# Stick-breaking attention: masks added by TensorE, logs summed as two float32r parts by single products

## The chip, the cores and the metric

The kernel runs on one core of a Trainium2 chip. The metric is the device time of one execution in microseconds (us). Three executions of the kernel before took 1486.97, 1491.43 and 1493.3 us; the median is 1491.43 us. The row tables and the trace come from one more execution under the profiler: 1495.53 us, of which the instructions span 1494.1 us, so 1.4 us lie around the span.

## The reference, cut to what matters

Two transformer blocks on 256 tokens of width 1024 are computed. The change touches one part of the first block, the stick-breaking attention of 16 heads of dimension 64. Its core is

```python
z = einsum('bhtd,bhsd->bhts', q * 64 ** -0.5, k)
causal = s < t                                  # strict
log_1mb = where(causal, log_sigmoid(-z), 0.0)
tail = cumsum(log_1mb, axis=s, reverse=True)
w = where(causal, exp(z + tail), 0.0)
out = einsum('bhts,bhsd->bhtd', w, v)
```

For each query t and key s the weight is exp of the score plus the sum of the logs of all keys from s to t. The work around it that matters here: the projections q, k, v before it, a gate projection `ga` of the same input that shares TensorE with the attention, and the projection `att` of the attention's output after it.

## The kernel before, in words

**Weights.** All weight matrices come in pieces of 128 x 2048 numbers. SyncE loads a piece into `raw` (4 slots); ScalarE rounds it to float32r (`w_hi`, `act_split`, L433); VectorE forms the rest, raw minus w_hi (`w_lo`, `dve_split`, L443); TensorE multiplies with three float32r products per tile (`three`, L453 to L455). Which engine splits which piece at which place is written out by hand in the program of each engine. Each engine runs its program in order, and semaphores (`wait_ge`, `then_inc`) are the only coupling.

**The attention stage** (`pe_stick`, `act_stick`, `dve_stick`) handles the 16 heads as 8 pairs j = 0 to 7, keys on the partitions, queries along the free axis. A pair's scores are 2 heads x 384 columns (key block 0 with 256 queries, key block 1 with the last 128), in PSUM, double buffered by `stick_z` (psum_a for even j, psum_c for odd j). For pair j:

1. TensorE, `pe_stick_scores`: four plain float32 products (L729, L730), once `stick_wt(j-2)` says that the PSUM buffer has been read out.
2. VectorE, L787: L = min(z, 30). ScalarE, L765 and L767: L = ln(1 + exp(L)). VectorE, L789: L = max(z, L). VectorE, L791: L times the strict mask on the two diagonal blocks.
3. TensorE, `pe_stick_weights`: six plain float32 products (L739 to L741) add to z the sums of L, with `neg_from` (lower triangle of -1) and `neg_ones` as weights of the products.
4. ScalarE, L773: `stick_w` = exp of PSUM. VectorE, L800, twice: min with 3e38 and strict mask on the diagonal blocks.
5. TensorE, `pe_stick_output`, L757: the product with v. ScalarE L779 and VectorE L806: the output in two float32r parts `y_hi` and `y_lo`.

The three programs interleave the pairs. In round j (1 to 6) TensorE does: one gate tile (12 products of `ga`), scores of pair j+1, one gate tile, weights of pair j, output of pair j-1. ScalarE does: exp and ln of pair j+1, in rounds 1, 2, 5 and 6 the split of one weight piece, the weights' exp of pair j, `y_hi` of pair j-1. VectorE does: min, max and mask of pair j+1, in the same rounds its half of the split, the weights' mask of pair j, `y_lo` of pair j-1. Ahead of round 4 ScalarE copies out the first half of the gate (`act_gate_out`, L911 and L912), for which TensorE waits before the first gate tile of that round.

**After the rounds** TensorE does weights(7), output(6), then the first half of `att0`, output(7), the rest of `att0` and then `att1`, which waits for splits that ScalarE starts after `y_hi(7)`, the second gate copy and the gate's sigmoid (L920).

**Before the stage** TensorE waits for the small column constants (`cols`, L705). VectorE then scales a few gain columns (L2951, L2957) and enters `dve_stick`. `memory_kv` is first written much later, by `kv2`.

Of the kernel before, what the change touches and what calls it, by code (L numbers as in the profile page):

```python
# [99 lines left out]
class Kernel:  # L100
# [9 lines left out]
    def memory(self):  # L110
# [28 lines left out]

        self.stage = self.put("stage", [P, 5, P], y_hi_at)  # L140
        half = 4 * KD * SEQ
        self.stick_l = self.put("stick_l", [P, 2, 2, 384], y_hi_at + half)
        self.stick_w = self.put("stick_w", [P, 2, 2, 384], y_lo_at + half)
        self.rows = self.put("rows", [P, 2, 4, 4, P], y_lo_at)
        self.xc = self.put("xc", [P, 2, MT, GH, SSM_HD], y_hi_at)
        self.xd = self.put("xd", [P, 2, GH, SSM_HD], y_hi_at + 8192)
# [180 lines left out]
    def semaphores(self, known):  # L327
        def new(name, unit=1):
            s = Signal(self.nc, self.ctx, name, known, unit)
            self.signals.append(s)  # L330
            return s
# [15 lines left out]
        self.res_added, self.post_sq_act, self.post_gain_dve, self.post_sums, self.post_mean, self.post_root = (  # L347
            new(n) for n in ("res_added", "post_sq_act", "post_gain_dve", "post_sums", "post_mean", "post_root"))

        (self.stick_z, self.stick_min, self.stick_exp, self.stick_ln, self.stick_max, self.stick_logs, self.stick_s, self.stick_wt,  # L350
         self.stick_wm, self.stick_o, self.stick_hi, self.stick_lo) = (new("stick_" + n) for n in (
             "z", "min", "exp", "ln", "max", "logs", "s", "wt", "wm", "o", "hi", "lo"))

        self.dt_act, self.dt_dve, self.conv_act, self.conv_dve, self.conv_silu, self.xs_turned, self.xs_act, self.xs_dve = (
            new(n) for n in ("dt_act", "dt_dve", "conv_act", "conv_dve", "conv_silu", "xs_turned", "xs_act", "xs_dve"))
# [358 lines left out]
def stick_z(k, j):  # L714

    return (k.psum_a, k.psum_c)[j % 2][:, 0:1024].rearrange("p (b w) -> p b w", b=2)[:, :, 0:384]


def stick_diagonal(x):
    return x.rearrange("p b (k t) -> p b k t", t=P)[:, :, 0:3:2, :]  # L720


def pe_stick_scores(k, j):
    pe, z = k.nc.tensor, stick_z(k, j)
    if j >= 2:
        pe.wait_ge(*k.stick_wt.by(j - 2))
    for b in range(2):
        r = slice(64 * b, 64 * b + 64)
        pe.matmul(z[:, b, 0:SEQ], k.k_t[r, j, 0:P], k.q_t[r, j, :], start=True, stop=False, skip_group_check=True)  # L729
        mm = pe.matmul(z[:, b, SEQ:384], k.k_t[r, j, P:SEQ], k.q_t[r, j, P:SEQ], start=False, stop=False, skip_group_check=True)  # L730
    mm.then_inc(*k.stick_z.at(j))


def pe_stick_weights(k, j):
    pe, z, u = k.nc.tensor, stick_z(k, j), j % 2
    pe.wait_ge(*k.stick_logs.by(j))
    for b in range(2):
        L = k.stick_l[:, u, b, :]
        pe.matmul(z[:, b, 0:SEQ], k.neg_from[:], L[:, 0:SEQ], start=False, stop=False, skip_group_check=True)  # L739
        pe.matmul(z[:, b, P:SEQ], k.neg_ones[:], L[:, SEQ:384], start=False, stop=False, skip_group_check=True)  # L740
        mm = pe.matmul(z[:, b, SEQ:384], k.neg_from[:], L[:, SEQ:384], start=False, stop=True, skip_group_check=True)  # L741
    mm.then_inc(*k.stick_s.at(j))


def stick_o(k, j):

    return k.psum_b[:, 512 * (j % 2):512 * (j % 2) + SEQ]


def pe_stick_output(k, j):  # L750
    pe, u, o = k.nc.tensor, j % 2, stick_o(k, j)
    pe.wait_ge(*k.stick_wm.by(j, 1))
    if j >= 2:
        pe.wait_ge(*k.stick_lo.by(j - 2))
    for m in range(MT):
        for b in range(2):
            mm = pe.matmul(o[64 * b:64 * b + 64, P * m:SEQ], k.v_n[:, m, j * P + 64 * b:j * P + 64 * b + 64],  # L757
                           k.stick_w[:, u, b, SEQ * m:SEQ * m + SEQ - P * m], start=m == 0, stop=m == 1, skip_group_check=True)
    mm.then_inc(*k.stick_o.at(j))


def act_stick_softplus(k, j):
    act, L = k.nc.scalar, k.stick_l[:, j % 2, :, :]
    act.wait_ge(*k.stick_min.by(j))
    act.activation(L, L, ACT.Exp).then_inc(*k.stick_exp.at(j))  # L765
    act.wait_ge(*k.stick_exp.by(j))
    act.activation(L, L, ACT.Ln, bias=1.0).then_inc(*k.stick_ln.at(j))  # L767


def act_stick_weights(k, j):  # L770
    act = k.nc.scalar
    act.wait_ge(*k.stick_s.by(j))
    act.activation(k.stick_w[:, j % 2, :, :], stick_z(k, j), ACT.Exp).then_inc(*k.stick_wt.at(j))  # L773


def act_stick_output(k, j):
    act = k.nc.scalar
    act.wait_ge(*k.stick_o.by(j))
    act.activation(k.Y[0][:, j, :], stick_o(k, j), ACT.Copy).then_inc(*k.stick_hi.at(j))  # L779


def dve_stick_softplus(k, j):

    dve, z, L = k.nc.vector, stick_z(k, j), k.stick_l[:, j % 2, :, :]
    strict = k.strict[:].unsqueeze(1).unsqueeze(1).to_broadcast([P, 2, 2, P])
    dve.wait_ge(*k.stick_z.by(j))
    dve.tensor_scalar(L, z, 30.0, None, ALU.min).then_inc(*k.stick_min.at(j))  # L787
    dve.wait_ge(*k.stick_ln.by(j))
    dve.tensor_tensor(L, z, L, ALU.max).then_inc(*k.stick_max.at(j))  # L789
    dve.wait_ge(*k.stick_max.by(j))  # L790
    dve.tensor_tensor(stick_diagonal(L), stick_diagonal(L), strict, ALU.mult).then_inc(*k.stick_logs.at(j))  # L791


def dve_stick_weights(k, j):
    dve = k.nc.vector
    strict = k.strict[:].unsqueeze(1).to_broadcast([P, 2, P])
    dve.wait_ge(*k.stick_wt.by(j))
    for b in range(2):
        d = stick_diagonal(k.stick_w[:, j % 2, b:b + 1, :])[:, 0, :, :]
        dve.scalar_tensor_tensor(out=d, in0=d, scalar=3.0e38, in1=strict, op0=ALU.min, op1=ALU.mult).then_inc(*k.stick_wm.at(j, b))  # L800
# [52 lines left out]
def act_stick(k):  # L853
    k.nc.scalar.preload_act_table_set("natural_log_exp_and_others")
    act_stick_softplus(k, 0)
    act_stick_softplus(k, 1)
    act_stick_weights(k, 0)
    for j in range(1, STICK - 1):
        if j == 4:
            act_gate_out(k, 0)  # L860
        act_stick_softplus(k, j + 1)
        if j in (1, 2, 5, 6):
            act_split(k, 1)
        act_stick_weights(k, j)
        act_stick_output(k, j - 1)
    act_stick_weights(k, STICK - 1)
    act_stick_output(k, STICK - 2)
    act_stick_output(k, STICK - 1)
    act_gate_out(k, 1)


def dve_stick(k):
    dve_stick_softplus(k, 0)
    dve_stick_softplus(k, 1)
    dve_stick_weights(k, 0)
    for j in range(1, STICK - 1):
# [2050 lines left out]
def vector_program(k):  # L2927
    dve, col = k.nc.vector, k.col_of
# [19 lines left out]
    for name, l, dim in (("fox_q_gain_2", 1, HD), ("mla_q_gain_2", 1, QK), ("mem_q_gain_2", 2, HD)):  # L2948
        c = HEAD_GAINS[name]
# [173 lines left out]
```

## Time and profile before

| what | value |
|---|---|
| three executions, median | 1491.43 us |
| profiled execution | 1495.53 us |
| its span | 1494.1 us |
| TensorE busy | 1358.6 us (91%) |
| VectorE busy | 907.2 us (61%) |
| ScalarE busy | 691.4 us (46%) |
| mean granted TensorE clock | 0.948 |

Busy time is summed per engine, and the engines run beside each other. PE is TensorE, PEld its weight loads, DVE is VectorE, ACT is ScalarE, POOL is GpSimd, SP is SyncE. In a row such as `L787 TENSOR_SCALAR stick_l<-psum_a 128x768`, the line of the kernel comes first, then the operation, what it writes and reads, and its size. A bracket `[1.88 <-PE psum_c L730]` at the end says how long the engine had been idle and what released it. A plain float32 product is recorded as two matmuls, so "x4" for L729 is two products.

### The profile page before, as it was taken

The page shows a single profiled execution, that of the slowest core. Times are in us where ns is not written, and L with a number is a line of the kernel's source. Part 1 is how long each engine was busy: PE and PEld are TensorE (multiplying, and loading weights), DVE is VectorE, ACT ScalarE, POOL GpSimd, SP SyncE. Part 2 cuts the span into 40 slices and gives each one's busy share as a digit, 9 for nine tenths or more (in the row PEclk, how much of TensorE's full clock was granted, in tenths as well). Part 3 has the DMA queues.
Part 4 walks back from the last instruction along what each step waited for, and adds up shares of the span by engine and source line. Part 5 has one row for each costly group of instructions (what it writes and reads, how often), then busy time and mean ns, then how long its engine had stood idle before and what let it go on. Part 6 is the DMA issues. An engine that isn't in the chain of part 4 may idle for free.

```text
span 1494.1 us, 21370 instructions
## 1 busy us (share of the span) xinstructions
PE 1358.6 (91%) x8820; PEld 1211.9 (81%) x8820; DVE 907.2 (61%) x1295; ACT 691.4 (46%) x974; POOL 156.1 (10%) x262
## 2 busy tenths in 40 slices
PE   5999998779998988899998899799997858899998
PEld 5988998448997987799997677699996746799997
DVE  4456478655646644654545666677766478576765
ACT  4345556225625444544333554545454456445442
POOL 6000020110000000020000131000000172000000
PEclk9999999779999999899999899899998869999999
DMA  7531444103653543356565433265663320266561
GB/s 263 177 131 35 169 170 170 57 0 113 231 206 114 188 151 99 113 176 198 177 186 182 141 113 85 71 200 181 182 192 127 134 57 15 85 182 198 171 191 63
DMA packets 206400, 212.68 MB, mean 142 GB/s; under 512 B 7009, under 2 KB 151859, under 8 KB 206304
## 3 DMA queue, kind: packets, MB, share of 16 engines
q1 hardware_dynamic: 203840, 206.25, 43.2%
q0 software_dynamic: 2160, 4.02, 0.8%
q8 instruction: 70, 1.15, 0.3%
q10 hardware_dynamic: 304, 1.05, 0.2%
q14 instruction: 26, 0.21, 0.0%
HBM read 210.24 MB, written 1.05 MB: 141 GB/s over the span
## 4 chain that ended last, share of the span: by engine, by line
PE 81%; DVE 10%; ACT 5%; issue 2%; POOL 1%; DMA 0%; DVEq 0%; ACTq 0%; POOLq 0%
PE psum_a L453 10%; PE psum_b L453 10%; PE psum_a L454 10%; PE psum_a L455 10%; PE psum_b L455 10%; PE psum_b L454 10%; PE psum_c L453 5%; PE psum_c L454 4%; PE psum_c L455 4%; DVE w_lo L443 3%; PE psum_c L571 2%; ACT w_hi L433 1%; PE psum_c L1139 1%; PE psum_c L1166 1%; ACT normed_rows L554 1%
## 5 line engine op out<-in xcount | busy, mean ns | idle before, releaser
L443 DVE TENSOR_TENSOR w_lo<-raw,w_hi 128x2048 fp32r<-128x2048 f32 (+3 forms) x235 | 447.8, 1942 | 94.7 <-ACT w_hi L433 93.9
L433 ACT ACTIVATE w_hi<-raw 128x2048 fp32r<-128x2048 f32 (+3 forms) x235 | 371.8, 1620 | 32.7 <-PE psum_b L455 18.0
L453 PE MATMUL psum_a<-x_hi,w_hi 128*128 128x256 f32 x752 | 215.9, 287 | 4.8 <-DVE w_lo L443 4.8
L454 PE MATMUL psum_a<-x_lo,w_hi 128*128 128x256 f32 x752 | 214.8, 286 | 0.0
L455 PE MATMUL psum_a<-x_hi,w_lo 128*128 128x256 f32 x752 | 214.7, 285 | 0.0
L453 PE MATMUL psum_b<-x_hi,w_hi 128*128 128x256 f32 x752 | 214.2, 285 | 0.0
L455 PE MATMUL psum_b<-x_hi,w_lo 128*128 128x256 f32 x752 | 213.6, 284 | 0.0
L454 PE MATMUL psum_b<-x_lo,w_hi 128*128 128x256 f32 x752 | 213.5, 284 | 0.0
L453 PEld LDWEIGHTS psum_a<-x_hi,w_hi 128*128 128x128 f32 x752 | 146.7, 195 | 6.3 <-DVE w_lo L443 5.1
L454 PEld LDWEIGHTS psum_a<-x_lo,w_hi 128*128 128x128 f32 x752 | 146.6, 195 | 1.4
L454 PEld LDWEIGHTS psum_b<-x_lo,w_hi 128*128 128x128 f32 x752 | 145.2, 193 | 1.6
L455 PEld LDWEIGHTS psum_a<-x_hi,w_lo 128*128 128x128 f32 x752 | 146.4, 195 | 0.0
L453 PEld LDWEIGHTS psum_b<-x_hi,w_hi 128*128 128x128 f32 x752 | 145.3, 193 | 1.4
L455 PEld LDWEIGHTS psum_b<-x_hi,w_lo 128*128 128x128 f32 x752 | 145.1, 193 | 0.0
L453 PE MATMUL psum_c<-w_hi,ffn_hidden_hi 128*128 128x512 f32 x264 | 106.2, 402 | 4.1 <-DVE ffn_hidden_lo L1582 4.1
L454 PE MATMUL psum_c<-w_lo,ffn_hidden_hi 128*128 128x512 f32 x264 | 105.6, 400 | 0.0
L455 PE MATMUL psum_c<-w_hi,ffn_hidden_lo 128*128 128x512 f32 x264 | 105.6, 400 | 0.0
L1590 POOL CAST ffn_hidden_hi<-ffn_h 128x256 fp32r<-128x256 f32 x66 | 26.5, 402 | 543.2 <-DVE ffn_h L1579 369.1
L571 PE MATMUL psum_c<-ident,normed_rows 128*128 128x128 f32 x144 | 32.2, 410 | 49.1 <-ACT normed_rows L554 45.2
L571 PEld LDWEIGHTS psum_c<-ident,normed_rows 128*128 128x128 f32 x144 | 23.7, 206 | 58.0 <-DVE normed_rows L548 29.2
L453 PEld LDWEIGHTS psum_c<-w_hi,ffn_hidden_hi 128*128 128x128 f32 x264 | 50.6, 192 | 14.3 <-issue 4.9
L455 PEld LDWEIGHTS psum_c<-w_hi,ffn_hidden_lo 128*128 128x128 f32 x264 | 50.4, 191 | 12.5
(495 smaller groups left out, 2594.8 us busy)
## 6 DMA issues: line engine op xcount, KB each, us to landing
raw<-in_ffn_w_up_dram SPq DMA_DIRECT2D x88, 512.0 KB, 5.1
raw<-in_w_in_dram SPq DMA_DIRECT2D x40, 1024.0 KB, 5.9
raw<-in_w_gu_dram SPq DMA_DIRECT2D x44, 512.0 KB, 5.1
raw<-in_ffn_w_down_dram SPq DMA_DIRECT2D x44, 512.0 KB, 5.9
raw<-in_w_down_dram SPq DMA_DIRECT2D x22, 512.0 KB, 5.9
raw<-in_w_br_ssm_dram SPq DMA_DIRECT2D x8, 1024.0 KB, 5.6
raw<-in_w_xkv_dram SPq DMA_DIRECT2D x8, 1024.0 KB, 5.7
raw<-in_w_out_dram SPq DMA_DIRECT2D x8, 1024.0 KB, 5.1
```

The source lines that it names most:

```text
L433: act.activation(k.w_hi[:, s, 0:size], k.raw[:, s, 0:size], ACT.Copy).then_inc(*k.rounded.at(*key))
L443: dve.tensor_tensor(k.w_lo[:, s, 0:size], k.raw[:, s, 0:size], k.w_hi[:, s, 0:size].bitcast(F32), ALU.subtract).then_inc(*k.split.at(*key))
L453: pe.matmul(out_ap, l[0], r[0], start=start, stop=False, skip_group_check=True)
L454: pe.matmul(out_ap, l[0], r[1], start=False, stop=False, skip_group_check=True)
L455: return pe.matmul(out_ap, l[1], r[0], start=False, stop=stop, skip_group_check=True)
L554: act.activation(k.normed_rows[:, 0, :], src[:, 0, :], ACT.Copy, scale=k.squares[:, at + 2:at + 3]).then_inc(*k.scaled_act.at(tag))
L571: mm = pe.transpose(ps[:, m * P:(m + 1) * P], k.normed_rows[:, m, j * P:(j + 1) * P], k.ident[:])
L1139: pe.matmul(ssd_seg(k, q), k.beyond[:], k.rows[:, g % 2, 2 * c + q, :, :].rearrange("p h t -> p (h t)"), start=True, stop=True).then_inc(* ...
L1166: mm = pe.matmul(k.psum_c[:, at:at + SSM_HD], k.rows[:, g % 2, 2 * c + q, h, :], k.xc[:, g % 2, c, 4 * q + h, :], start=q == 0 and h == 0, ...
L1590: pool.tensor_copy(k.hid[0][:, u, :], k.h32[:, u, :]).then_inc(*k.ffn_hi.at(tag, h))
```

## The change

It changes how pairs are masked and how the logs are summed.

- **Constants.** Four 128 x 128 float32r tiles `stick_consts` (copies of `neg_from`, `neg_ones`, `ident`, and a tile of 0 and -1e30 made from `strict`) are written by VectorE ahead of `dve_stick`. TensorE waits for them ahead of its stage.
- **Scores.** Four float32r products of 128 columns, identity times mask tile, are added to the scores of each pair, and `stick_z` is signalled behind them. The maskings L791 and L800 are gone.
- **Logs.** After max, ScalarE copies L (128 x 768) to a float32r tile `stick_l_hi` (`act_stick_logs`), then VectorE writes `stick_l_lo` = L - `stick_l_hi` (128 x 768). The copy stands in ScalarE's program right behind the pair's ln, ahead of the round's split and of the weights' exp.
- **Sums.** Six plain float32 products per pair become eight float32r ones: 4 of 384 columns and 4 of 128.
- **Buffers.** `stick_l` has one buffer in place of two (in the place of `memory_kv`), so min(j) waits for the logs of j-1. `stick_w` moves, and its exp waits for output(j-2).

```diff
 def pe_stick_scores(k, j):
...
-        mm = pe.matmul(z[:, b, SEQ:384], k.k_t[r, j, P:SEQ], k.q_t[r, j, P:SEQ], start=False, stop=False, skip_group_check=True)
+        pe.matmul(z[:, b, SEQ:384], k.k_t[r, j, P:SEQ], k.q_t[r, j, P:SEQ], start=False, stop=False, skip_group_check=True)
+    for b in range(2):
+        for at in (0, SEQ):
+            mm = pe.matmul(z[:, b, at:at + P], k.stick_consts[:, 2, :], k.stick_consts[:, 3, :], start=False, stop=False,
+                           skip_group_check=True)
     mm.then_inc(*k.stick_z.at(j))
...
-        L = k.stick_l[:, u, b, :]
-        pe.matmul(z[:, b, 0:SEQ], k.neg_from[:], L[:, 0:SEQ], start=False, stop=False, skip_group_check=True)
-        pe.matmul(z[:, b, P:SEQ], k.neg_ones[:], L[:, SEQ:384], start=False, stop=False, skip_group_check=True)
-        mm = pe.matmul(z[:, b, SEQ:384], k.neg_from[:], L[:, SEQ:384], start=False, stop=True, skip_group_check=True)
+        for part in k.stick_parts:
+            pe.matmul(z[:, b, 0:384], k.stick_consts[:, 0, :], part[:, u, b, :], start=False, stop=False, skip_group_check=True)
+        for part in k.stick_parts:
+            mm = pe.matmul(z[:, b, P:SEQ], k.stick_consts[:, 1, :], part[:, u, b, SEQ:384], start=False, stop=True,
+                           skip_group_check=True)
...
-    pe.wait_ge(*k.stick_wm.by(j, 1))
+    pe.wait_ge(*k.stick_wt.by(j))
...
+def act_stick_logs(k, j):
+    act, u = k.nc.scalar, j % 2
+    act.wait_ge(*k.stick_max.by(j))
+    if j >= 2:
+        act.wait_ge(*k.stick_s.by(j - 2))
+    act.activation(k.stick_parts[0][:, u, :, :], k.stick_l[:, :, :], ACT.Copy).then_inc(*k.stick_logs_hi.at(j))
...
 def dve_stick_softplus(k, j):
...
+    if j:
+        dve.wait_ge(*k.stick_logs.by(j - 1))
     dve.tensor_scalar(L, z, 30.0, None, ALU.min).then_inc(*k.stick_min.at(j))
     dve.wait_ge(*k.stick_ln.by(j))
     dve.tensor_tensor(L, z, L, ALU.max).then_inc(*k.stick_max.at(j))
-    dve.wait_ge(*k.stick_max.by(j))
-    dve.tensor_tensor(stick_diagonal(L), stick_diagonal(L), strict, ALU.mult).then_inc(*k.stick_logs.at(j))
+    dve.wait_ge(*k.stick_logs_hi.by(j))
+    dve.tensor_tensor(k.stick_parts[1][:, u, :, :], L, k.stick_parts[0][:, u, :, :].bitcast(F32), ALU.subtract).then_inc(*k.stick_logs.at(j))
...
 def act_stick(k):
     k.nc.scalar.preload_act_table_set("natural_log_exp_and_others")
     act_stick_softplus(k, 0)
+    act_stick_logs(k, 0)
     act_stick_softplus(k, 1)
+    act_stick_logs(k, 1)
     act_stick_weights(k, 0)
     for j in range(1, STICK - 1):
         if j == 4:
             act_gate_out(k, 0)
         act_stick_softplus(k, j + 1)
+        act_stick_logs(k, j + 1)
         if j in (1, 2, 5, 6):
             act_split(k, 1)
         act_stick_weights(k, j)
```

`dve_stick` loses its calls of `dve_stick_weights` and is otherwise as before.

## Rows read from the trace of the kernel before

**Rows 1.** Page, the chain that ended last, its shares by engine.

```profile
PE 81%; DVE 10%; ACT 5%; issue 2%; POOL 1%; DMA 0%; DVEq 0%; ACTq 0%; POOLq 0%
```

**Rows 2.** Chain in time order, attention stage: start, duration (us), work.

```profile
103.67 1.91 ACT w_hi L433
105.60 2.29 DVE w_lo L443
107.89 0.67 DVE stick_w L800 x2
```

**Rows 3.** Timeline of DVE: start, duration (us), instruction, idle before and releaser.

```profile
90.99 0.23 DVE L2957 TENSOR_TENSOR head_cols<-head_cols 128x1 f32<-128x1 f32 x2
91.70 0.96 DVE L787 TENSOR_SCALAR stick_l<-psum_a 128x768 f32<-128x768 f32 x1 [0.49 <-PE psum_a L730]
96.05 0.95 DVE L787 TENSOR_SCALAR stick_l<-psum_c 128x768 f32<-128x768 f32 x1
98.79 0.96 DVE L789 TENSOR_TENSOR stick_l<-psum_c,stick_l 128x768 f32<-128x768 f32 x1 [1.79 <-ACT stick_l L767]
99.78 0.69 DVE L791 TENSOR_TENSOR stick_l<-stick_l,strict 128x512 f32<-128x512 f32 x1
101.06 0.95 DVE L787 TENSOR_SCALAR stick_l<-psum_a 128x768 f32<-128x768 f32 x1
108.48 0.41 DVE L806 TENSOR_TENSOR y_lo<-psum_b,y_hi 128x256 fp32r<-128x256 f32 x1
108.81 0.95 DVE L787 TENSOR_SCALAR stick_l<-psum_c 128x768 f32<-128x768 f32 x1
116.56 0.95 DVE L787 TENSOR_SCALAR stick_l<-psum_a 128x768 f32<-128x768 f32 x1
123.86 0.96 DVE L787 TENSOR_SCALAR stick_l<-psum_c 128x768 f32<-128x768 f32 x1 [1.88 <-PE psum_c L730]
130.51 0.96 DVE L787 TENSOR_SCALAR stick_l<-psum_a 128x768 f32<-128x768 f32 x1 [1.23 <-PE psum_a L730]
138.28 0.95 DVE L787 TENSOR_SCALAR stick_l<-psum_c 128x768 f32<-128x768 f32 x1
```

**Rows 4.** Timeline of ACT in the same stage.

```profile
97.03 0.84 ACT L765 ACTIVATE stick_l<-stick_l 128x768 f32<-128x768 f32 x1 [2.62 <-DVE stick_l L787]
97.91 0.84 ACT L767 ACTIVATE stick_l<-stick_l 128x768 f32<-128x768 f32 x1
98.66 0.79 ACT L773 ACTIVATE stick_w<-psum_a 128x768 f32<-128x768 f32 x1
105.47 0.79 ACT L773 ACTIVATE stick_w<-psum_c 128x768 f32<-128x768 f32 x1
119.17 0.79 ACT L773 ACTIVATE stick_w<-psum_c 128x768 f32<-128x768 f32 x1
```

**Rows 5.** Timeline of PE: the stage, then the first att1 product and a later mask product.

```profile
121.26 0.39 PE L453 MATMUL psum_c<-x_hi,w_hi 128*128 128x256 f32 x1 [2.10 <-ACT merged L912]
122.87 0.71 PE L729 MATMUL psum_c<-q_t,k_t 64*128 64x256 f32 x4
144.19 0.60 PE L739 MATMUL psum_c<-stick_l,neg_from 128*128 128x256 f32 x2
146.03 0.87 PE L757 MATMUL psum_b<-stick_w,v_n 128*64 128x256 f32 x8
146.84 0.39 PE L453 MATMUL psum_a<-y_hi,w_hi 128*128 128x256 f32 x1
162.54 0.39 PE L453 MATMUL psum_b<-y_hi,w_hi 128*128 128x256 f32 x1 [2.97 <-DVE w_lo L443]
879.56 0.67 PE L2168 MATMUL psum_c<-causal_r,ident_r 128*128 128x128 f32 x4
```

**Rows 6.** Windows: length; busy us of PE, PEld, DVE, ACT, POOL; granted clock; DMA.

```profile
160.00:162.00 2.00, 0.00 (x0) 0.00 (x0) 1.80 (x1) 2.00 (x3) 0.00 (x0) 1.00 0.00 0
164.00:166.00 2.00, 2.00 (x12) 2.00 (x11) 2.00 (x4) 0.00 (x0) 0.00 (x0) 0.50 0.88 319
```

More of the change, by code:

```diff
@@ L134, in memory @@
         self.rotary = self.sb("rotary", [P, 2, MT, 16])
+        self.memory_kv_at = self.top
         self.memory_kv = self.sb("memory_kv", [P, MT, 2 * MEM_W])
@@ L141, in memory @@
         half = 4 * KD * SEQ
-        self.stick_l = self.put("stick_l", [P, 2, 2, 384], y_hi_at + half)
-        self.stick_w = self.put("stick_w", [P, 2, 2, 384], y_lo_at + half)
         self.rows = self.put("rows", [P, 2, 4, 4, P], y_lo_at)
@@ L156, in memory @@
         self.v_n = self.put("v_n", [P, MT, D], at + 24576)
+        self.stick_parts = [self.put(n, [P, 2, 2, 384], o, F32R)
+                            for n, o in (("stick_l_hi", at + 32768), ("stick_l_lo", y_lo_at + half))]
+        self.stick_w = self.put("stick_w", [P, 2, 2, 384], y_hi_at + half)
+        self.stick_l = self.put("stick_l", [P, 2, 384], self.memory_kv_at)
+        self.stick_consts = self.put("stick_consts", [P, 4, P], at + 38912, F32R)
         self.gate_s = self.put("gate_s", [P, KD, SEQ], at + 8192)
@@ L348, in semaphores @@
             new(n) for n in ("res_added", "post_sq_act", "post_gain_dve", "post_sums", "post_mean", "post_root"))
-        (self.stick_z, self.stick_min, self.stick_exp, self.stick_ln, self.stick_max, self.stick_logs, self.stick_s, self.stick_wt,
-         self.stick_wm, self.stick_o, self.stick_hi, self.stick_lo) = (new("stick_" + n) for n in (
-             "z", "min", "exp", "ln", "max", "logs", "s", "wt", "wm", "o", "hi", "lo"))
+        (self.stick_z, self.stick_min, self.stick_exp, self.stick_ln, self.stick_max, self.stick_logs_hi, self.stick_logs, self.stick_s,
+         self.stick_wt, self.stick_o, self.stick_hi, self.stick_lo, self.stick_made) = (new("stick_" + n) for n in (
+             "z", "min", "exp", "ln", "max", "logs_hi", "logs", "s", "wt", "o", "hi", "lo", "made"))
         self.dt_act, self.dt_dve, self.conv_act, self.conv_dve, self.conv_silu, self.xs_turned, self.xs_act, self.xs_dve = (
@@ L716, in stick_z, with dve_stick_consts @@
     return (k.psum_a, k.psum_c)[j % 2][:, 0:1024].rearrange("p (b w) -> p b w", b=2)[:, :, 0:384]
-def stick_diagonal(x):
-    return x.rearrange("p b (k t) -> p b k t", t=P)[:, :, 0:3:2, :]
+def dve_stick_consts(k):
+    dve, c = k.nc.vector, k.stick_consts
+    for j, x in enumerate((k.neg_from, k.neg_ones, k.ident)):
+        dve.tensor_copy(c[:, j, :], x[:])
+    dve.tensor_scalar(c[:, 3, :], k.strict[:], 1.0, -NEG, ALU.subtract, ALU.mult).then_inc(*k.stick_made.at())
 def pe_stick_scores(k, j):
@@ L762, in act_stick_softplus @@
 def act_stick_softplus(k, j):
-    act, L = k.nc.scalar, k.stick_l[:, j % 2, :, :]
+    act, L = k.nc.scalar, k.stick_l[:, :, :]
     act.wait_ge(*k.stick_min.by(j))
@@ L772, in act_stick_weights @@
     act.wait_ge(*k.stick_s.by(j))
+    if j >= 2:
+        act.wait_ge(*k.stick_o.by(j - 2))
     act.activation(k.stick_w[:, j % 2, :, :], stick_z(k, j), ACT.Exp).then_inc(*k.stick_wt.at(j))
@@ L782, in dve_stick_softplus @@
 def dve_stick_softplus(k, j):
-    dve, z, L = k.nc.vector, stick_z(k, j), k.stick_l[:, j % 2, :, :]
-    strict = k.strict[:].unsqueeze(1).unsqueeze(1).to_broadcast([P, 2, 2, P])
+    dve, z, u = k.nc.vector, stick_z(k, j), j % 2
+    L = k.stick_l[:, :, :]
     dve.wait_ge(*k.stick_z.by(j))
+    if j:
+        dve.wait_ge(*k.stick_logs.by(j - 1))
     dve.tensor_scalar(L, z, 30.0, None, ALU.min).then_inc(*k.stick_min.at(j))
@@ L789, in dve_stick_softplus @@
     dve.tensor_tensor(L, z, L, ALU.max).then_inc(*k.stick_max.at(j))
-    dve.wait_ge(*k.stick_max.by(j))
-    dve.tensor_tensor(stick_diagonal(L), stick_diagonal(L), strict, ALU.mult).then_inc(*k.stick_logs.at(j))
[L794 to L800, printed above, removed]
+    dve.wait_ge(*k.stick_logs_hi.by(j))
+    dve.tensor_tensor(k.stick_parts[1][:, u, :, :], L, k.stick_parts[0][:, u, :, :].bitcast(F32), ALU.subtract).then_inc(*k.stick_logs.at(j))
 def dve_stick_output(k, j):
@@ L813, in pe_stick @@
         k.nc.tensor.wait_ge(*k.out_dve.by(unit))
+    k.nc.tensor.wait_ge(*k.stick_made.by())
     gates = pe_gate_tiles(k)
@@ L874, in dve_stick @@
     dve_stick_softplus(k, 1)
-    dve_stick_weights(k, 0)
     for j in range(1, STICK - 1):
@@ L879, in dve_stick @@
             dve_split(k, 1)
-        dve_stick_weights(k, j)
         dve_stick_output(k, j - 1)
-    dve_stick_weights(k, STICK - 1)
     dve_stick_output(k, STICK - 2)
@@ L2957, in vector_program @@
         dve.tensor_tensor(k.head_cols[:, c:c + 1], k.head_cols[:, a:a + 1], k.head_cols[:, b:b + 1], ALU.mult).then_inc(*k.scaled_gains.at(c))
+    dve_stick_consts(k)
     dve_stick(k)
```

## The prediction

> **What bounds the kernel now.** I read the chain that ended last first: TensorE has 81% of it, VectorE 10%, ScalarE 5%, DMA 0% [rows 1]. Nothing waits for data from memory, so what a stage loses on its own chain reaches the end. Then I read the chain in order of time inside the stage that the diff touches (about 91 to 147 us). There it isn't TensorE throughout: in a round with a weight split it goes through ScalarE's split, VectorE's split and VectorE's masking of the weights [rows 2]. The timeline of VectorE shows the beat of the stage. I call m(j) the start of min(j), L787. It stands at 91.70, 96.05, 101.06, 108.81, 116.56, 123.86, 130.51 and 138.28 us for j = 0 to 7 [rows 3]. Steps between them: 4.35, 5.01, 7.75, 7.75, 7.30, 6.65, 7.77. The split rounds (7.75) are VectorE's: its instructions follow each other without an idle bracket. The steps 7.30 and 6.65 end in a wait for the scores, so TensorE sets them, the first of the two through its wait of 2.10 us for the gate's copy [rows 3, 5]. From m(7) to the first `att0` product it is 146.84 - 138.28 = 8.56 us [rows 3, 5].
>
> **Prices of what moves.**
> *Scores.* From the first score product to min it is 123.86 - 122.87 = 0.99 us [rows 3, 5]. Four float32r mask products come in between. The same product stands in the fox stage: four take 0.67 us from the first start to the last end, which is 0.17 each if nothing overlaps, and (0.67 - 0.39) / 3 = 0.09 for each further one if a single one lasts 0.39 like the L453 row [rows 5]. I take 0.13, the middle: four are 0.5 us (bounds 0.37 and 0.67), and scores to min becomes 1.49.
> The Trainium skill, "TensorE: Matmul & The Clock Gate", section "Back-to-back issue gap", gives about 81 ns for each 128-column product with its weight load. By it the four would be 0.32 us, an estimate; the trace's four float32r products are slower than that, and the measured row is used.
> *Sums.* The six float32 products take 146.03 - 144.19 = 1.84 us [rows 5]. The gate tile, twelve float32r products of 256 columns, takes 122.87 - 121.26 = 1.61, so 0.13 each, as for 128 columns; 384 columns lie between 0.13 and 0.20 (half as much again), and I take 0.17. Four of each kind: 4 x 0.17 + 4 x 0.13 = 1.2, with the tail 1.3 us. TensorE saves 0.54 a pair here and pays 0.5 for the masks: its own work stays the same.
> *VectorE.* Gone per pair: mask of L, at most 0.69 us, and mask of the weights, 0.67 [rows 2, 3]. New: the subtraction of 128 x 768, at 0.96 like L789 of the same size, 0.87 until the next can start. In sum 0.4 less.
> *ScalarE.* New: a copy of 128 x 768, 0.84 like L765, 0.75 until the next starts (98.66 - 97.91) [rows 4].
>
> **Where they lie.** The copy needs max(j), and in ScalarE's program the split and the weights' exp stand behind it. From m: exp at +0.98, ln at +1.86, max at +2.74, the dependent instruction at +3.73 (99.78 - 98.79 = 0.99 later) [rows 3, 4]. Before, ScalarE was free for the split at m+2.61. Now the copy runs at +3.73 and ScalarE is free at +4.48: the split and the exp are 1.87 us later, behind a wait for VectorE's max. The subtraction starts at +4.6, and the logs are there at +5.6.
> - *Split round.* ScalarE's split starts at +4.48 and takes 1.91; VectorE's split starts at +6.4 and holds VectorE 2.2 (105.60 to 107.8) [rows 2]; y_lo takes 0.33 more (108.48 to 108.81) [rows 3]. Next min at +8.94, not 7.75: +1.19 for each of four (m2 to m3, m3 to m4, m6 to m7; the fourth split falls behind m7). VectorE's saved masks are hidden, because it now idles for ScalarE's half. Scores would be there at +4.48 + 1.80 + 0.79 + 0.05 + 1.49 = 8.6, just inside.
> - *Round without split.* Exp of the weights at +4.48, done at +5.27, scores at +5.31, next min at +6.80. For m5 to m6 that is +0.15 over 6.65. For m1 to m2 the same loop, 6.80 for 5.01: +1.79.
> - *m0 to m1.* Min(1) waits for the subtraction of pair 0: +5.6 for 4.35: +1.24.
> - *m4 to m5.* Exp of the weights at +4.48; in the trace it was at +2.61 (119.17 - 116.56), and the gate tile, the scores and min hung on it through y_hi and the gate copy. Everything shifts by 1.87, with the masks' 0.5: +2.36.
> - *Entry.* The constants are four VectorE instructions of 128 x 128 behind L2957, which ends at 91.22. Each costs between the 0.1 of a tiny one (0.23 for two) and 0.69 for 128 x 512 [rows 3]; I take 0.22, so TensorE starts at about 92.1 in place of 90.74 (0.96 ahead of 91.70, as above): +1.35. With the masks m0 is 1.85 later. Bounds 0.9 to 3.2.
> - *Exit.* From m7: scores(7) had started 1.82 before m7 (at m6 + 7.12), then TensorE needs scores 1.4, gate 1.45, sums 1.3, output 0.81, two gate tiles 2.95, sums(7) 1.3 and output(6) 0.81, in sum 10.0, so `att0` starts at m7+8.2 in place of 8.56: -0.36.
>
> Sum: 1.85 + 1.24 + 1.79 + 3 x 1.19 + 2.36 + 0.15 - 0.36 = 10.6 us later at `att0`. Behind it, the chain y_hi(7), gate copy, sigmoid, split of `att1` hangs on output(7), which moves with `att0`, so all 10.6 pass on; the single L buffer and the waits for output(j-2) and s(j-2) are met long before and cost nothing.
>
> **The clock.** TensorE's work per round is about 6.6 us, so in the longer rounds it idles 2.3 to 3.1 us at a stretch. In the trace an idle stretch of 2.97 us ahead of 162.54 was followed by a granted clock of 0.50 at 164 to 166 us, the level of 1.2 GHz, with 12 products in 2 us where 0.13 us each gives 15 [rows 5, 6]. Idle 2.10 us ahead of 121.26 did no harm that I see. If a fall lands on the gate tile and scores of m4 to m5, or on scores(2), it is on the chain; in the split rounds 0.3 us of slack covers part. I put 1.2 us on it, bounds 0 and 8. Forecast: 10.6 + 1.2 = +11.8 us. Against the profiled execution that is 1495.53 + 11.8 = 1507.3; the profiled execution lies 4.1 above the median of the three, so the time is 1491.4 + 11.8 = 1503.2 us.
>
> **Rivals.**
> A. *VectorE's load decides, not the order on ScalarE*, the case on the other side. If the copy slipped in beside other work (ScalarE is idle 2.6 us ahead of L765 [rows 4]), the split rounds would fall by the 0.4 that VectorE saves, and the stage would change by 1.85 - 3 x 0.4 = +0.6, less if the entry is hidden: 1492, within 0.5%. Against it: that idle time lies before min, and the copy needs max. It decides from the point at which ScalarE's copy ends before its split could start anyway, and the code's order excludes that. Chance 0.13.
> B. *Faster*: float32r takes the sums off TensorE as if TensorE were the bound of every round. Eight pairs times 0.54 give -4.3 if the masks hide under them; masks and entry take back 5.9. Only with nearly free masks and constants does it give 1488. 1483 would need more than the whole of the sums' 1.84 us a pair to come free. Chance 0.05, and I count 0.03 of it beyond 0.5%, for what I may have overlooked.
> C. *The clock falls in each long gap.* Five gaps (before scores(2), (3), (4), the gate tile, scores(7)), each losing up to half of 3 us = 1.5 us on the chain, 7.5 in all: 10.6 + 7.5 = +18, 1509.5 us. For it: the row of the fall; against: slack in the split rounds, and the price is full only when the fall starts with the scores. The Trainium skill, "TensorE: Matmul & The Clock Gate", section "HAM oscillation — how this bites in real kernels", tells of a loop whose every burst restarts cold because a wait precedes it; by that rule C would be the case, and the one fall behind 162.54 agrees with it. Chance 0.17.
> The forecast has 0.65.
>
> **How the numbers follow.** The forecast's own spread is about 3 us each way: entry bounds, mask price, and executions of before that differ by 6 us. The range for 8 in 10 is 1496.5 to 1511. It leaves out most of A and B and the upper edge of C. About 0.5%, 7.5 us, is what a measurement can tell from no change, so the border to slower is 1498.9. Of the forecast's 0.65 some 0.07 fall short of it, C's 0.17 lie above: slower 0.75. A's 0.13, 0.02 of B and that 0.07: same 0.22. Faster 0.03.
>
> **What would show it.** In the timeline of the changed kernel: ScalarE's Copy of stick_l_hi starting 3.7 us behind min and released by max; the w_hi split behind it; VectorE idle 1 us or more before w_lo with ScalarE as releaser; steps between mins near 8.9 (split), 6.8, and 9.7 for m4 to m5; the sums at 1.2 to 1.3 us; mask products at 0.13 each; the first `att0` product near 157.5 us. Wrong if the split rounds stay at 7.75 or less, or if scores and not VectorE release min there.

## The result

The changed kernel takes 1509.05 us (median of 7 executions, 1499.97 to 1510.04) against 1491.43 us before (median of 7 too, 1486.97 to 1493.30). The medians differ by 17.6 us. The estimated ratio of the two kernels is 1.0106, with a 95% interval of 1.0084 to 1.0128, so the changed one is slower by 12.5 to 19.1 us, middle 15.8. The forecast was 1503.2 us in a range of 1496.5 to 1511. The profiled execution took 1507.57 us (span 1506.2 us), 12.0 more than that of before; both had a mean granted clock of 0.948.

VectorE of the changed kernel, one min (now L814) per pair, with the copy that starts the stage and one round in full (start, duration in us, instruction, idle before and releaser):

```profile
89.01 0.74 DVE L710 COPY cols<-psum_c 128x563 f32<-128x563 f32 x1
92.59 0.96 DVE L814 TENSOR_SCALAR stick_l<-psum_a 128x768 f32<-128x768 f32 x1 [1.71 <-PE psum_a L743]
98.27 0.96 DVE L814 TENSOR_SCALAR stick_l<-psum_c 128x768 f32<-128x768 f32 x1
106.04 0.96 DVE L814 TENSOR_SCALAR stick_l<-psum_a 128x768 f32<-128x768 f32 x1 [2.20 <-PE psum_a L743]
110.66 0.96 DVE L818 TENSOR_TENSOR stick_l_lo<-stick_l,stick_l_hi 128x768 fp32r<-128x768 f32 x1 [0.91 <-ACT stick_l_hi L790]
112.46 2.29 DVE L448 TENSOR_TENSOR w_lo<-raw,w_hi 128x2048 fp32r<-128x2048 f32 x1 [0.85 <-ACT w_hi L438]
115.00 0.95 DVE L814 TENSOR_SCALAR stick_l<-psum_c 128x768 f32<-128x768 f32 x1
123.96 0.94 DVE L814 TENSOR_SCALAR stick_l<-psum_a 128x768 f32<-128x768 f32 x1
135.21 0.96 DVE L814 TENSOR_SCALAR stick_l<-psum_c 128x768 f32<-128x768 f32 x1 [5.26 <-PE psum_c L743]
142.11 0.96 DVE L814 TENSOR_SCALAR stick_l<-psum_a 128x768 f32<-128x768 f32 x1 [0.89 <-PE psum_a L743]
151.08 0.95 DVE L814 TENSOR_SCALAR stick_l<-psum_c 128x768 f32<-128x768 f32 x1
```

The mins stand 5.68, 7.77, 8.96, 8.96, 11.25, 6.90 and 8.97 us apart, where before they stood 4.35, 5.01, 7.75, 7.75, 7.30, 6.65 and 7.77 apart [rows 3]. The round in full shows why: VectorE idles 0.91 us for ScalarE's copy and 0.85 for ScalarE's split, where before the split followed the mask without an idle bracket:

```profile
105.60 2.29 DVE L443 TENSOR_TENSOR w_lo<-raw,w_hi 128x2048 fp32r<-128x2048 f32 x1
```

ScalarE of the changed kernel in the same round, the copy and the split behind it:

```profile
109.78 0.85 ACT L790 ACTIVATE stick_l_hi<-stick_l 128x768 fp32r<-128x768 f32 x1 [1.02 <-DVE stick_l L816]
110.53 1.90 ACT L438 ACTIVATE w_hi<-raw 128x2048 fp32r<-128x2048 f32 x1
```

The copy starts 109.78 - 106.04 = 3.74 us behind min, the split at 4.49. TensorE of the changed kernel, its longer waits, the masks (L743), the sums (L753) with the output behind them, and the first `att0` product:

```profile
91.03 0.71 PE L739 MATMUL psum_a<-q_t,k_t 64*128 64x256 f32 x4 [2.06 <-DVE stick_consts L730]
103.60 0.93 PE L739 MATMUL psum_a<-q_t,k_t 64*128 64x256 f32 x4 [2.54 <-ACT stick_w L798]
113.17 0.71 PE L739 MATMUL psum_c<-q_t,k_t 64*128 64x256 f32 x4 [1.51 <-ACT stick_w L798]
114.03 0.66 PE L743 MATMUL psum_c<-stick_consts 128*128 128x128 f32 x4
122.13 0.71 PE L739 MATMUL psum_a<-q_t,k_t 64*128 64x256 f32 x4 [2.44 <-ACT stick_w L798]
130.52 0.39 PE L458 MATMUL psum_c<-x_hi,w_hi 128*128 128x256 f32 x1 [3.49 <-ACT merged L931]
149.25 0.71 PE L739 MATMUL psum_c<-q_t,k_t 64*128 64x256 f32 x4 [2.18 <-ACT stick_w L798]
152.09 0.34 PE L753 MATMUL psum_a<-stick_l_hi,stick_consts 128*128 128x384 f32 x1
153.28 0.87 PE L772 MATMUL psum_b<-stick_w,v_n 128*64 128x256 f32 x8
159.04 0.38 PE L458 MATMUL psum_a<-y_hi,w_hi 128*128 128x256 f32 x1
```

From the start of the cols copy to the first `att0` product it is 70.03 us (159.04 - 89.01). Before it was 146.84 - 89.89 = 56.95:

```profile
89.89 0.74 DVE L705 COPY cols<-psum_c 128x563 f32<-128x563 f32 x1
```

The stage costs 13.1 us; I use this measure, which doesn't depend on when the stage begins, for all kernels. Two windows of the changed kernel in which the clock was at or near its lower level (columns as in [rows 6]):

```profile
104.00:106.00 2.00, 2.00 (x13) 1.71 (x10) 0.00 (x0) 0.00 (x0) 0.00 (x0) 0.50 0.04 8
131.00:133.00 2.00, 2.00 (x13) 1.77 (x13) 0.00 (x0) 0.00 (x0) 0.00 (x0) 0.57 0.03 8
```

Both falls follow waits of the TensorE rows (2.54 and 3.49 us), and both lie where scores or gate tile are on the chain.

### The profile page after: what moved, and what is told of

Read it like the earlier page. It is cut to its first block, busy times and chain, and to the rows that moved or that the text cites. A ratio compares the mean times of both kernels' runs of the same rounds, so it can differ in the third digit from the quotient of the medians.

```text
span 1506.2 us, 21385 instructions
## 1 busy us (share of the span) xinstructions
PE 1359.6 (90%) x8820; PEld 1213.9 (81%) x8820; DVE 904.7 (60%) x1283; ACT 697.6 (46%) x982; POOL 156.0 (10%) x262
## 4 chain that ended last, share of the span: by engine, by line
PE 80%; DVE 10%; ACT 6%; issue 2%; POOL 1%; DMA 0%; DVEq 0%; ACTq 0%; POOLq 0%
PE psum_a L458 10%; PE psum_b L458 10%; PE psum_a L460 10%; PE psum_a L459 10%; PE psum_b L460 9%; PE psum_b L459 9%; PE psum_c L458 4%; PE psum_c L459 4%; PE psum_c L460 4%; DVE w_lo L448 2%; PE psum_c L576 2%; ACT w_hi L438 1%; PE psum_c L1158 1%; PE psum_c L1185 1%; ACT normed_rows L559 1%
## 5 line engine op out<-in xcount | busy, mean ns | idle before, releaser
L460 PEld LDWEIGHTS psum_c<-w_hi,ffn_hidden_lo 128*128 128x128 f32 x264 | 50.5, 191 | 12.5
```

The costliest lines, as they stand in the source:

```text
L460: return pe.matmul(out_ap, l[1], r[0], start=False, stop=stop, skip_group_check=True)
```

## The experiments

All ratios are to the kernel before, on the same chip. "Stage" is the time from the cols copy to the first `att0` product in the profiled execution. The diffs below are cut to the lines that matter and shortened by "..."; they are against the changed kernel.

| kernel | stage, us | ratio | 95% interval |
|---|---|---|---|
| before | 56.95 | 1 | |
| changed | 70.03 | 1.0106 | 1.0084 to 1.0128 |
| masks only | 59.29 | 1.0034 | 1.0015 to 1.0053 |
| parts only | 78.70 | 1.0146 | 1.0120 to 1.0172 |
| split first | 71.40 | 1.0087 | 1.0063 to 1.0111 |
| gaps filled | 69.29 | 1.0085 | 1.0058 to 1.0111 |
| masks, lean | 55.11 | 0.9982 | 0.9966 to 0.9998 |
| overlapped parts | 59.12 | 1.0007 | 0.9993 to 1.0022 |
| gate copy moved | 56.00 | 0.9998 | 0.9985 to 1.0010 |
| changed, second trace | 70.05 | 1.0113 | 1.0079 to 1.0146 |
| changed, third trace | 69.95 | one execution | |
| before, second trace | 58.48 | one execution | |

**Half the change: masks only.**

```diff
-        for part in k.stick_parts: ...                     # eight float32r products
+        pe.matmul(z[:, b, 0:SEQ], k.neg_from[:], L[:, 0:SEQ], ...)   # six float32 products, as before
-    dve.wait_ge(*k.stick_logs_hi.by(j))
-    dve.tensor_tensor(k.stick_parts[1][:, u, :, :], L, ...)
-    act_stick_logs(k, j + 1)                               # at every place
```

> Half of the change: masks by TensorE as in the changed kernel (with its constants), sums again as six plain float32 products of an L with two buffers, no copy and no subtraction. Theory 1 (the copy in ScalarE's order is the cost): split rounds at 7.15 us from min to min, now TensorE's own work (6.65 + 0.5), against 8.96 in the changed kernel; entry +1.8, m0 to m1 -0.7, three split rounds -0.6 each, the two rounds without split and the exit +0.5 each: about +0.7 us on before, ratio 1.000 within 0.002. Theory 2 (the masks on TensorE are the cost, through scores to min and TensorE's load): about as slow as the changed kernel, ratio 1.006 or more.

Mins of this kernel:

```profile
108.86 0.96 DVE L801 TENSOR_SCALAR stick_l<-psum_c 128x768 f32<-128x768 f32 x1
115.98 0.96 DVE L801 TENSOR_SCALAR stick_l<-psum_a 128x768 f32<-128x768 f32 x1
124.62 0.96 DVE L801 TENSOR_SCALAR stick_l<-psum_c 128x768 f32<-128x768 f32 x1 [3.75 <-PE psum_c L741]
```

Split rounds take 7.12 us, as theory 1 said, and the stage 2.3 us more than before instead of 0.7: the step m4 to m5 came at 8.64, not 7.8, and the exit at 9.56, 1.0 us more than before and not 0.5. The timed ratio, 1.0034, lies just above the 1.002 that I had allowed and below the 1.006 of theory 2. By themselves the masks and their constants cost 2.3 us of stage; theory 2 fails as the main cause.

**The other half: parts only.**

```diff
+    dve.tensor_tensor(stick_diagonal(L), stick_diagonal(L), strict, ALU.mult).then_inc(*k.stick_masked.at(j))
-    act.wait_ge(*k.stick_max.by(j))
+    act.wait_ge(*k.stick_masked.by(j))                     # in act_stick_logs
-            mm = pe.matmul(z[:, b, at:at + P], k.stick_consts[:, 2, :], k.stick_consts[:, 3, :], ...)
+        dve_stick_weights(k, j)                            # as before
```

> The other half: float32r parts by copy and subtraction and eight float32r products, both maskings by VectorE as before. Theory 1: the copy now waits for max and mask, so ScalarE's split starts 5.2 us behind min and a split round takes 10.3 us; summed over entry, eight steps and exit +18 us, with falls of the clock +21, ratio 1.012 to 1.016, slower than the whole change. Theory 2: without the masks it is faster than the changed kernel, ratio 1.005 or less.

```profile
107.41 0.96 DVE L815 TENSOR_SCALAR stick_l<-psum_a 128x768 f32<-128x768 f32 x1 [0.74 <-PE psum_a L745]
117.77 0.95 DVE L815 TENSOR_SCALAR stick_l<-psum_c 128x768 f32<-128x768 f32 x1
```

A split round takes 10.36 us (10.3 expected) and the stage 21.8 us more than before (21). With the masks on TensorE the same parts cost less: the copy no longer waits for VectorE's mask. So the larger cost comes with the copy and the subtraction. The halves don't add up to the whole (2.3 and 21.8 against 13.1 us): both write the constants, whose entry is 1.8 and 1.9 us longer than before, and in the parts-only kernel the copy waits for one instruction more.

**Is it the order on ScalarE? Split ahead of the copy.**

```diff
         act_stick_softplus(k, j + 1)
-        act_stick_logs(k, j + 1)
         if j in (1, 2, 5, 6):
             act_split(k, 1)
+        act_stick_logs(k, j + 1)
```

VectorE's split goes ahead of its subtraction in the same way.

> The changed kernel with ScalarE's split ahead of the copy, and VectorE's split ahead of the subtraction, in rounds 1, 2, 5 and 6. Theory 1: ScalarE's split starts 2.6 us behind min instead of 4.5; split rounds take 7.95 us instead of 8.96, four of them 4 us less than the changed kernel, ratio to before about 1.007. Rival (the copy's and subtraction's length decides, wherever they stand): split rounds stay at 8.9 and the ratio at 1.0106.

Mins, and the wait of TensorE ahead of sums(7), and the clock behind the wait for the gate:

```profile
114.37 0.96 DVE L814 TENSOR_SCALAR stick_l<-psum_c 128x768 f32<-128x768 f32 x1 [0.19 <-issue]
122.33 0.95 DVE L814 TENSOR_SCALAR stick_l<-psum_a 128x768 f32<-128x768 f32 x1
```

```profile
158.25 0.44 PE L753 MATMUL psum_c<-stick_l_hi,stick_consts 128*128 128x384 f32 x1 [1.76 <-DVE stick_l_lo L822]
```

```profile
130.00:138.00 8.00, 8.00 (x38) 7.39 (x38) 1.72 (x2) 1.69 (x2) 0.00 (x0) 0.51 0.01 2
```

The split rounds fall to 7.96 (122.33 - 114.37; m2 to m3 took 8.24), as theory 1 said. So 1.0 of the 1.2 us that such a round had become longer is the order. The rest stays: VectorE's subtraction now stands between its split and `y_lo`, on the path to the next min, and without it the masks-only kernel takes 7.12. But the stage is 1.4 us longer in this trace, not 4 shorter: the late subtraction makes TensorE wait 1.76 us at the exit, and the clock stays at its lower level through 130 to 138 us, so that m4 to m5 takes 12.17 and m5 to m6 8.03. The ratio, 1.0087, can't be told from that of the changed kernel. The order sets the split rounds; what moving it alone gained there was lost elsewhere.

**The clock: products of a zero tile in two gaps.**

```diff
+        if j == 4:
+            k.nc.tensor.wait_ge(*k.stick_lo.by(1))
+            for _ in range(24):
+                k.nc.tensor.matmul(k.psum_b[:, 768:1024], k.stick_zero[:], k.X[0][:, 0, :], start=False, ...)
         next(gates)
+        if j == 1:
+            for _ in range(16):
+                k.nc.tensor.matmul(k.psum_c[:, 1024:1280], k.stick_zero[:], k.X[0][:, 0, :], start=False, ...)
         pe_stick_scores(k, j + 1)
```

> The changed kernel with products of a zero tile in the two gaps that a fall of the clock followed: 16 ahead of scores(2), added to the open gate sums, and 24 ahead of the gate tile of round 4, into unused columns. Clock theory: no fall of the granted clock between 91 and 160 us; the steps m1 to m2 and m4 to m5 take 6.8 and 9.7 us instead of 7.77 and 11.25, 2.5 us less in the profile, and the timed runs come 3 to 6 us below the changed kernel, ratio 1.007 to 1.009. Rival (falls elsewhere or nothing): steps as in the changed kernel, ratio 1.0106.

```profile
98.39 0.96 DVE L816 TENSOR_SCALAR stick_l<-psum_c 128x768 f32<-128x768 f32 x1
105.29 0.96 DVE L816 TENSOR_SCALAR stick_l<-psum_a 128x768 f32<-128x768 f32 x1 [1.32 <-PE psum_a L745]
```

```profile
146.98 0.71 PE L741 MATMUL psum_c<-q_t,k_t 64*128 64x256 f32 x4 [2.17 <-ACT stick_w L800]
```

```profile
148.00:150.00 2.00, 2.00 (x11) 2.00 (x12) 1.75 (x3) 0.21 (x1) 0.00 (x0) 0.53 0.14 22
```

The two steps came at 6.90 and 9.75 us instead of 7.77 and 11.25: 2.4 us were the clock's. But "no fall between 91 and 160 us" was wrong. The clock fell elsewhere: to 0.50 at 114 to 116 us behind a gap of 2.18 us (1.51 in the changed kernel), and to 0.53 at 148 to 150 us behind a gap of 2.17 us, which had the same length in the changed kernel (2.18) without a fall. The second came ahead of the exit, which took 9.49 us instead of 7.96. The stage gained 0.7 us only.

**Repairs of the masks-only kernel.** One mask product of 256 columns per head, constants ahead of VectorE's copy of v1, and the first gate copy ahead of the weights' exp of pair 3:

```diff
-        for at in (0, SEQ):
-            mm = pe.matmul(z[:, b, at:at + P], k.stick_consts[:, 2, :], k.stick_consts[:, 3, :], ...)
+        blocks = z[:, b, :].rearrange("p (c t) -> p c t", t=P)[:, 0:3:2, :]
+        mm = pe.matmul(blocks, k.stick_consts[:, 2, :], k.stick_consts[:, 3:4, :].to_broadcast([P, 2, P]), ...)
-        if j == 4:
-            act_gate_out(k, 0)
+        if j == 3:
+            act_gate_out(k, 0)                             # ahead of act_stick_weights(k, 3)
```

> Masks by TensorE, sums as six plain float32 products (as e1), with three repairs: one float32r product of 256 columns per head in place of two of 128, the constants written by VectorE during an earlier wait (ahead of its copy of v1), the first gate copy ahead of the weights' exp of pair 3. Theory (TensorE's work sets the stage once the copy is gone): it does 0.25 us a pair more than before and recovers the waits of 2.1 and 1.0 us and VectorE's masking; the first att0 product comes 1 to 2 us earlier than before, counted from the end of the cols copy; ratio 0.998 to 1.001. If it were still VectorE or ScalarE, split rounds would stay at 7.75 and the ratio at 1.001 or more.

```profile
108.21 0.95 DVE L801 TENSOR_SCALAR stick_l<-psum_c 128x768 f32<-128x768 f32 x1
115.29 0.95 DVE L801 TENSOR_SCALAR stick_l<-psum_a 128x768 f32<-128x768 f32 x1
```

The stage is 1.8 us shorter than before, and the timed ratio 0.9982 (0.9966 to 0.9998). This version beats both kernels, the one before by 0.2%, at the edge of what the measurement resolves. Split rounds take 7.08. The constants now lie ahead of the cols copy, so what they cost there is outside this measure; the timed ratio includes it.

**Repairs of the parts.** On ScalarE the copy goes behind the weights' exp, L has two buffers, GpSimd subtracts for pairs 2 to 7, and the three repairs above are in:

```diff
         act_stick_weights(k, j)
+        act_stick_logs(k, j + 1)
         act_stick_output(k, j - 1)
...
+    for j in range(2, STICK):
+        stick_low(k, k.nc.gpsimd, j)
```

> The changed kernel's two parts and masks, but with the copy behind the split and the weights' exp on ScalarE, two buffers of L, the subtraction on GpSimd for pairs 2 to 7, and the three repairs of e5. Theory 1 (the order was the cost, not the work): split rounds fall to 7.1 us (VectorE: min, max, split, y_lo), the round without split to 6.2 (TensorE), no wait of TensorE ahead of round 4; first att0 product 4 to 6 us earlier than before from the cols copy, ratio 0.996 to 0.999. Rival (float32r parts cost more than they save wherever they stand, or GpSimd is too late with the subtraction): TensorE waits for it ahead of the sums, split rounds above 7.75, ratio 1.002 or more.

Two mins, GpSimd's subtraction, TensorE's wait at the exit, and the clock behind it:

```profile
110.14 0.95 DVE L814 TENSOR_SCALAR stick_l<-psum_c 128x768 f32<-128x768 f32 x1
117.22 0.95 DVE L814 TENSOR_SCALAR stick_l<-psum_a 128x768 f32<-128x768 f32 x1
```

```profile
122.40 1.84 POOL L825 TENSOR_TENSOR stick_l_lo<-stick_l,stick_l_hi 128x768 fp32r<-128x768 f32 x1 [3.71 <-ACT stick_l_hi L790]
143.33 2.47 POOL L825 TENSOR_TENSOR stick_l_lo<-stick_l,stick_l_hi 128x768 fp32r<-128x768 f32 x1 [4.54 <-ACT stick_l_hi L790]
```

```profile
145.86 0.44 PE L753 MATMUL psum_c<-stick_l_hi,stick_consts 128*128 128x384 f32 x1 [1.79 <-POOL stick_l_lo L825]
```

```profile
148.00:150.00 2.00, 2.00 (x13) 1.48 (x10) 0.42 (x1) 0.77 (x2) 0.00 (x0) 0.50 0.00 0
```

The rounds fell as theory 1 said (7.08 with a split, 6.26 for m5 to m6), and the stage takes 59.12 us: 10.9 of the 13.1 us are gone. It isn't shown that all of that was the order, because this kernel also takes the subtraction off VectorE, gives L a second buffer and has the three repairs. The fair comparison is the kernel with the same repairs and no parts, whose stage is 4.0 us shorter (55.11). There the rival was right, at two places. At the start m0 to m1 takes 5.49 us against 3.62, and m1 to m2 5.48 against 5.01. At the exit nothing covers ScalarE's copy and GpSimd's 2.47 us, the clock falls to 0.50 behind the wait of 1.79 us, and `att0` starts 11.63 us behind m7, against 9.30 there and 8.56 before. Only m5 to m6 gains (6.26 against 6.90). The ratio is 1.0007, neither of the two that were expected. The work that float32r saves on TensorE didn't pay for the start and the exit.

**The gate copy alone.** The kernel before with only that move:

> The kernel before with one move: the first gate copy ahead of the weights' exp of pair 3. TensorE's wait of 2.10 us ahead of round 4 should go; the step m4 to m5 falls from 7.30 to about 6.7, and since TensorE then has work in every round the first att0 product comes 0.5 to 2 us earlier, ratio 0.999 to 1.000. If the exp, one us later, delays the scores of pair 5 instead, nothing is gained.

```profile
116.79 0.95 DVE L787 TENSOR_SCALAR stick_l<-psum_a 128x768 f32<-128x768 f32 x1
123.13 0.96 DVE L787 TENSOR_SCALAR stick_l<-psum_c 128x768 f32<-128x768 f32 x1 [0.83 <-PE psum_c L730]
```

The step m4 to m5 fell from 7.30 to 6.34 and the stage by 0.95 us; TensorE's wait ahead of round 4 fell from 2.10 to 1.13 us; I had expected it to go. The ratio of 0.9998 doesn't resolve it.

**Second and third traces.** The changed kernel twice more and the kernel before once more, nothing edited.

> The changed kernel again, for a second trace. Clock theory: the steps that no fall touches repeat to 0.1 us (5.7, then split rounds at 8.96, 6.9), while the falls of the clock lie elsewhere; from cols copy to first att0 product 68.0 us without any fall on the chain, up to 73 with several; the first trace had 70.0. Rival (a fixed cost that I don't see): 70.0 again, with the same two falls.

> The changed kernel, a third trace. Clock theory: untouched steps repeat to 0.1 us and from cols copy to first att0 product it takes between 68 and 73 us, by where the falls lie; rival: 70.0 with the same two falls.

> The kernel before again, for a second trace. Clock theory: no fall between the cols copy and the first att0 product, and the same 56.9 us between them within 0.2; its time lies with the mean clock (1491 at 0.952, 1496 at 0.948), that is, what varies lies outside this stage.

The stage of the changed kernel took 70.05 and 69.95 us, with the same two falls at 104 and 131 us: here the rival was right, and my expectation that the falls would wander inside the stage wrong. The kernel before did vary, against my expectation of 56.9 within 0.2: 58.48 us in its second trace, with a fall (0.50 at 122 to 124 us) behind the 2.09 us wait for the gate, and m4 to m5 at 8.64:

```profile
120.56 0.39 PE L453 MATMUL psum_c<-x_hi,w_hi 128*128 128x256 f32 x1 [2.09 <-ACT merged L912]
```

```profile
115.87 0.95 DVE L787 TENSOR_SCALAR stick_l<-psum_a 128x768 f32<-128x768 f32 x1
124.51 0.96 DVE L787 TENSOR_SCALAR stick_l<-psum_c 128x768 f32<-128x768 f32 x1 [3.22 <-PE psum_c L730]
```

What varies most lies far behind the stage. The same two instructions of GpSimd in the second trace of the changed kernel (clock 0.952, 1500.65 us) and in the third (0.948, 1507.77 us):

```profile
505.26 0.69 POOL L547 TENSOR_TENSOR squares<-squares,half_neg 128x2 f32<-128x2 f32 x1 [4.14 <-DVE squares L541]
1159.56 0.70 POOL L547 TENSOR_TENSOR squares<-squares,half_neg 128x2 f32<-128x2 f32 x1 [7.66 <-DVE squares L541]
```

```profile
503.88 0.69 POOL L547 TENSOR_TENSOR squares<-squares,half_neg 128x2 f32<-128x2 f32 x1 [4.14 <-DVE squares L541]
1166.72 0.70 POOL L547 TENSOR_TENSOR squares<-squares,half_neg 128x2 f32<-128x2 f32 x1 [9.20 <-DVE squares L541]
```

Between these two points one execution of the same program takes 8.5 us longer (662.84 against 654.30). One difference among several is a fall at 541 us. The first window is the second trace, the next one the third:

```profile
541.00:543.00 2.00, 1.62 (x10) 1.04 (x11) 2.00 (x6) 2.00 (x6) 0.00 (x0) 1.00 0.00 0
```

```profile
541.00:543.00 2.00, 2.00 (x11) 1.73 (x10) 1.89 (x6) 1.83 (x5) 0.00 (x0) 0.53 0.00 0
```

Taken over all twelve traces, what lies behind the stage has two lengths. From the first `att0` product to the end of the span it takes 1340.2 to 1342.2 us in six of them and 1345.3 to 1348.3 us in the other six, in no order of kernels: the first traces of the kernel before and of the changed kernel are long (1347.3 and 1347.2), the second trace of the changed kernel is short (1340.2) and its third long (1347.3). The fall at 541 us doesn't tell the two lengths apart: counted from the first `att0` product, five of the six short traces have one at that place too. A fall some 40 us later (mean clock 0.83 at 580 to 590 us in the third trace) is in all six long traces and in none of the short ones.

## Why the prediction was right, and where it was off

The mechanism of the stage was right, and most terms held, here in the order of the sum (expected, then measured in us):

| term | expected | measured |
|---|---|---|
| entry | 1.85 | 1.77 |
| m0 to m1 | 1.24 | 1.33 |
| m1 to m2 | 1.79 | 2.76 |
| three split rounds | 3 x 1.19 | 1.21, 1.21, 1.20 |
| m4 to m5 | 2.36 | 3.95 |
| m5 to m6 | 0.15 | 0.25 |
| exit | -0.36 | -0.60 |
| clock | 1.2 | in the steps above, 2.4 |
| sum | 11.8 | 13.1 |

- *Prices.* Sums: 153.28 - 152.09 = 1.19 us for 1.3. Masks: scores to min went from 0.99 to about 1.56 (0.5 expected, 0.57 measured, from 91.03 to 92.59 in the entry). The copy and the subtraction took the 0.85 and 0.96 of their neighbours.
- *The clock.* The mis-sized term of the stage. The filled gaps put it at 0.87 + 1.5 = 2.4 us against 1.2. Without it m1 to m2 is 1.9 longer than before (1.79 expected) and m4 to m5 2.45 (2.36 expected), so 10.7 us are left where the sum had 10.6. Falls followed waits of 2.54 and 3.49 us; I had taken 2.97 as the nearest row of a fall and counted a part only.
- *Rival C*, a fall in each long gap, happened in two gaps of five; none followed the waits of 2.44 and 2.18 us. Its time, 1509.5 us, is nearer to the measured 1509.05 than the forecast is, but by luck: it put 18 us into the stage, which cost 13.1.
- *Rival A* (VectorE's load decides) is refuted by the idle brackets of 0.91 and 0.85 us. Its price was wrong too: with the copy out of the way of ScalarE's split, split rounds took 7.96 us and not 7.35, since the saved mask of L had been hidden beside ScalarE's split, and the subtraction, 0.87 us to the next start, takes the place of the mask of the weights, 0.67.
- *Rival B* (faster) is refuted by the result, and by the parts-only kernel, in which the float32r sums with their copy and subtraction alone came to a ratio of 1.0146.
- *A reading that was wrong.* Before the change VectorE's instructions in a split round don't all follow each other without an idle bracket: in every round it waits 1.8 us for ScalarE's ln ahead of max, as the row at 98.79 shows [rows 3]. Such a round is a chain through both engines and not VectorE's load. The sum followed the chain, so the slip cost nothing there.
- *From the stage to the whole.* The step that was off most is this one: the sum was added to the median of before as if the rest stood still. Between the two first traces it did: from the cols copy to the end of the span the changed kernel takes 13.0 us longer, so the stage's loss reaches the end in full. The profiled times differ by 12.0 only because its cols copy starts 0.9 us earlier. That the forecast for the profiled execution, 1507.3 us, meets the measured 1507.57 so closely is luck: a stage 1.3 us dearer than forecast and this earlier start nearly cancel.
- *Why the medians differ by more.* The timed executions don't stand still. Of the 60 timed executions of before, ten took 1495 to 1498 us (at a clock of 0.948) and the others 1487 to 1494, most of them at 0.952; of the twelve of the changed kernel in its two timed sets, ten took 1507.6 to 1510 us at a clock of 0.941 to 0.949 and two took 1500 (0.948 and 0.952). Long against long that is about 12, short against short about 9 to 12. If these are the two lengths that the traces show, 7 us apart, the mix is worth about (10/12 - 10/60) x 7 = 4.7 us, an estimate from these counts, and 13.0 + 4.7 is close to the 17.6 between the medians. That the timed groups are those of the traces is argued and not shown, and why the changed kernel lands in the longer one more often is open. The measured time lies in the range, 2 us below its upper edge.

## What to carry to other kernels

Before a small instruction goes onto an engine that looks idle, find what it waits for and what stands behind it in that engine's program. Here 0.85 us of copy, with a subtraction behind it, cost 1.2 us in each split round; 1.0 of it went when the split stood ahead of the copy, which waits for VectorE. Put such work behind what others wait for, and see who covers it in the first and the last round, where little or nothing is left to overlap. Idle time that a longer beat gives TensorE can be paid a second time when the clock falls on the work that follows the wait: 2.4 of the 13.1 us here. Sub-percent differences need several timed executions of both kernels; one execution of each under the profiler differed by 12.0 us where the medians said 17.6.

## What the hardware showed that I had not expected

- Filling the gaps that a fall had followed moved the falls to other gaps: 2.18 us of waiting ahead of scores(7) did no harm in the changed kernel, and 2.17 us at the same place was followed by a clock of 0.53 in the kernel with filled gaps. In the kernel before, the same wait for the gate (2.10 and 2.09 us) was followed by a fall in one trace and not in the other.
- GpSimd's subtraction of 128 x 768 took 1.82 and 1.84 us with VectorE idle for much of it, and 2.36 to 2.54 us in the rounds in which VectorE's split ran beside it; VectorE takes 0.96.
- VectorE's four instructions for the constants (128 x 128 each) took 0.22 us each but started 0.13 to 0.14 us apart.
- What lies behind the stage took one of two lengths, 1340.2 to 1342.2 or 1345.3 to 1348.3 us, whatever the kernel, in single executions of a program on one core.
